# Routing of a mixture of experts: logits in four column groups, folded as they are turned, and the token rows turned back beside the picking

## The chip, the cores and the metric

The kernel runs on one core of a Trainium2 chip. The time is the device time of one execution in microseconds (us), the median of several. All data is 32-bit floating point. The names of the engines in the profile are PE (TensorE; PEld is its loading of weights), ACT (ScalarE), DVE (VectorE), POOL (GpSimd) and SP (SyncE).

## The reference

The program is two transformer layers over 256 latent and 256 context tokens of 1024 features, and then two hybrid layers over the 256 latent ones. Each of the first two layers ends in a mixture of 16 experts. This is the part that the change touches:

```python
def moe(h, router_w, router_b, w1, w3, w2):
    N = h.shape[0]
    scores = jax.nn.sigmoid((h @ router_w).astype(jnp.float32))
    sel = (scores + router_b.astype(jnp.float32)).reshape(N, N_GROUPS, EXP_PER_GROUP)
    group_score = lax.top_k(sel, TOP_K)[0].sum(axis=-1)
    g_idx = jnp.argmax(group_score, axis=-1)
    sel_in = jnp.take_along_axis(sel, g_idx[:, None, None], axis=1)[:, 0]
    _, local = lax.top_k(sel_in, TOP_K)
    e_idx = g_idx[:, None] * EXP_PER_GROUP + local
    w = jnp.take_along_axis(scores, e_idx, axis=-1)
    w = w / w.sum(axis=-1, keepdims=True)
    comb = (jax.nn.one_hot(e_idx, N_EXPERTS, dtype=jnp.float32) * w[..., None]).sum(axis=1).astype(h.dtype)
    y = jnp.zeros_like(h)
    for e in range(N_EXPERTS):
        y = y + comb[:, e:e + 1] * ((jax.nn.silu(h @ w1[e]) * (h @ w3[e])) @ w2[e])
    return y
```

There are 4 groups of 4 experts, and each token goes to 2 experts of its best group. In the first layer all 512 tokens pass through the experts, in the second the 256 latent ones.

## The kernel before

**Stages.** The program is written as stages (`class Stage`, L110 to L148). In a stage each engine has a program of its own; each waits at its start until every engine that took part in the stages before has finished (`stage_done`), so no two stages overlap. Within a stage, engines meet through counting semaphores: `bank_full` (a PSUM bank is written), `bank_free_act` (ScalarE has emptied one), `act_out` (ScalarE has written a result). Inside one engine's program a `drain` waits until its own writes are visible.

**Layout.** `hT` holds the normalised and modulated activations with the features on the partitions: 8 tiles (`KT`) of 128 features by up to 512 tokens. `turn` (L266) turns tiles of 128x128 on TensorE, four into one PSUM bank, and ScalarE copies each bank out. A product in this data type is two MATMUL instructions in the trace, a transpose is one.

**The order around the change.** Ahead of the experts of each layer (`moe` at L452 for the first layer with `nt` = 4 tiles of tokens, `moe_narrow` at L730 for the second with `nt` = 2) stand:

1. `turned` (L438): `xn` is turned into `hT`.
2. `turn` once more: `hT` is turned back into `h_tok`, rows of tokens, in `2 * nt` banks.
3. `route` (L1051), its first stage. TensorE makes the logits in one bank for each tile of tokens: `hT` is stationary and `router_w` (128x16 for each `k`) moves, `nt * 8` products (L1088). ScalarE issues the stores of `h_tok` to `h_rows` in HBM (`keep_rows`, L482 and L760) and then takes the sigmoids (L1097). GpSimd makes small tables: `prio`, `iota`, `base`, `token` and the strict triangle `before`.
4. `route`, its second stage, on VectorE alone: some forty small steps from L1118 to L1159. They pick the best group, the best expert (`hot`) and the second (`hot2`), put their sum in `sel` (L1146), and compute the two weights.
5. `route`, its third stage. TensorE counts (L1169 and L1172): the rank of each token among those of its expert is the product of `before` with its own tile, plus the product of `ones` with each tile ahead of it; a further `nt` products give the total of each expert. VectorE (L1180 to L1199) takes from these `rank`, `first` and `passes`, the number of passes that the experts' loop makes.
6. The experts' stage. SyncE waits for `stage_done` of the routing before it requests any expert weights into the `ring` of 3 buffers. VectorE makes `picks` from `rank` (L692), TensorE multiplies them with `mine` for the indices of the tokens (L611), and GpSimd gathers the rows of each expert from `h_rows` (L637), for which it first waits on `h_stored`. Then the products run expert by expert (L585, L604).

**Elsewhere.** The modulation's products (`product`, L332) use `silu_c`, padded to 32 columns, as stationary tile. Product `k` writes the 32 partitions of PSUM that begin at `32 * (k % 4)`, so four products stand in four column groups of the array; `cond_of` (128x2, L189), a stack of four pieces of an identity, later adds the groups up (L359 and L362). At the start of the program ScalarE's queue issues the parameter loads (L205), ahead of its first activation (L407). The first product of the modulation waits for that.

The core of the counts before is:

```python
for m in range(nt):
    for b in range(m + 1):
        mm = pe.matmul(bank[0][:, m * N_EXP:(m + 1) * N_EXP], before[:, :] if b == m else ones[:, :],
                       sel[:, b, :], start=(b == 0), stop=(b == m))
for m in range(nt):
    mm = pe.matmul(bank[1][:, 0:N_EXP], ones[:, :], sel[:, m, :], start=(m == 0), stop=(m == nt - 1))
```

## Time and profile before

| what | value |
|---|---|
| median of three runs | 2834.15 us |
| lowest and highest run | 2834.11 and 2837.87 us |
| the profiled execution, its own time | 2837.68 us |
| its span | 2835.9 us |
| granted clock of TensorE, mean | 0.955 |
| DVE, ACT, POOL busy | 29%, 17%, 4% of the span |

The span is what the profiler sees of the execution; the 1.8 us around it belong to its time. The granted clock is a share of TensorE's full speed. It has two levels: 0.5 is 1.2 GHz and 1.0 is 2.4 GHz, and a value between them is a mean over a stretch with both. A timeline row gives the start, the length from the first start to the last end, and how many instructions it joins; what stands in brackets is idle time of that engine just before, and what ended it.

### The profile page before, as it was taken

What the parts mean: (1) busy time and instruction counts of PE and PEld (TensorE: products, weight loads), DVE (VectorE), ACT (ScalarE), POOL (GpSimd) and SP (SyncE); (2) the same over time, 40 slices, a digit from 0 to 9 for tenths busy, and PEclk for the clock granted to TensorE, in tenths of its full rate; (3) what the DMA queues carried; (4) which work ended last, traced back from release to release, by engine and by line L of the source; (5) the groups of instructions that cost most, each with busy time, mean ns of one, the idle gap of its engine ahead of it and who ended that gap; (6) DMA issues with size and microseconds to landing.
All of it is one profiled execution on the core that took longest, in us unless ns stands there. A gap on an engine that the chain in (4) does not pass through costs nothing.

```text
span 2835.9 us, 29978 instructions
## 1 busy us (share of the span) xinstructions
PE 2601.5 (92%) x12110; PEld 1746.6 (62%) x12110; DVE 830.0 (29%) x2043; ACT 478.9 (17%) x1010; POOL 113.2 (4%) x156
## 2 busy tenths in 40 slices
PE   5999998599997587799959999999999999999999
PEld 3465653444443245344424888888886788888884
DVE  0255321200100263111111677212210377512220
ACT  2133322111111222011110112101110111111210
POOL 0000000000000000000000000400000000400000
PEclk8999999699999797899979999999999999999999
DMA  7403483499997220999962443343443434344442
GB/s 240 127 30 104 145 294 125 152 329 330 336 334 261 101 69 15 320 384 385 380 253 95 148 137 131 139 157 120 149 162 120 153 125 143 119 149 141 149 148 96
DMA packets 299770, 517.14 MB, mean 182 GB/s; under 512 B 25072, under 2 KB 118640, under 8 KB 299632
## 3 DMA queue, kind: packets, MB, share of 16 engines
q1 hardware_dynamic: 281168, 473.87, 48.4%
q0 software_dynamic: 5824, 20.97, 2.1%
q10 hardware_dynamic: 12640, 20.37, 1.9%
q8 instruction: 97, 1.59, 0.2%
q14 instruction: 41, 0.34, 0.0%
HBM read 496.31 MB, written 18.87 MB: 182 GB/s over the span
## 4 chain that ended last, share of the span: by engine, by line
PE 85%; DMA 6%; DVE 3%; ACT 2%; ACTq 1%; issue 1%; DVEq 1%; POOL 0%; SPq 0%; POOLq 0%
PE bank L2536 32%; PE bank L585 8%; PE bank L2522 4%; DMA ring<-in_exp_w 4%; PE bank L604 4%; PE bank L1541 3%; PE bank L866 3%; PE bank L1551 3%; PE bank L2656 3%; PE bank L2671 3%; PE bank L1927 2%; PE bank L342 2%; PE bank L871 2%; PE bank L2021 1%; PE bank L2630 1%; PE bank L2620 1%
## 5 line engine op out<-in xcount | busy, mean ns | idle before, releaser
L2536 PE MATMUL bank<-hT,ring 128*128 128x256 f32 x3456 | 763.4, 381 | 7.0 <-DVE hT L2862 7.0
L2536 PEld LDWEIGHTS bank<-hT,ring 128*128 128x128 f32 x3456 | 655.1, 191 | 97.9 <-issue 10.4
L585 PE MATMUL bank<-ring,hg 128*128 128x512 f32 x512 | 226.9, 597 | 1.0 <-DVE hg L686 1.0
L2977 DVE SCALAR_TENSOR_TENSOR y_conf<-y_glu,s_cw,y_conf 128x256 f32<-128x256 f32 x480 | 195.0, 478 | 0.8
L585 PEld LDWEIGHTS bank<-ring,hg 128*128 128x128 f32 x512 | 95.7, 192 | 110.1 <-issue 110.1
L3059 DVE SCALAR_TENSOR_TENSOR y_conf<-bank,s_fw,y_conf 128x255 f32<-128x255 f32 (+1 forms) x176 | 72.7, 475 | 216.3 <-ACT y_conf L2805 214.3
L866 PE MATMUL bank<-ring,hg 128*64 128x512 f32 x512 | 119.8, 610 | 10.1 <-DMA ring<-in_exp_w 7.0
L2522 PE MATMUL bank<-ring,hT 128*128 128x512 f32 (+1 forms) x320 | 122.1, 545 | 6.6 <-DVE hT L2862 6.6
L604 PE MATMUL bank<-ring,hidT 128*128 128x512 f32 x256 | 112.6, 592 | 1.3 <-ACT hidT L667 1.3
L2522 PEld LDWEIGHTS bank<-ring,hT 128*128 128x128 f32 x320 | 57.6, 196 | 71.6 <-issue 69.9
L1541 PE MATMUL bank<-ring,hT 128*128 128x384 f32 (+2 forms) x256 | 97.9, 526 | 2.9 <-ACTq L132 2.9
L1551 PE MATMUL bank<-ring,hT 128*128 128x384 f32 (+2 forms) x256 | 95.8, 517 | 0.0
L604 PEld LDWEIGHTS bank<-ring,hidT 128*128 128x128 f32 x256 | 48.6, 190 | 62.2 <-issue 60.7
L866 PEld LDWEIGHTS bank<-ring,hg 128*64 128x64 f32 x512 | 36.6, 139 | 73.9 <-issue 69.7
L686 DVE COPY hg<-bank 128x512 f32<-128x512 f32 x32 | 20.7, 687 | 207.9 <-PE bank L571 207.9
L342 PE MATMUL bank<-ring,silu_c 128*32 128x512 f32 x384 | 52.1, 664 | 30.0 <-ACT silu_c L407 23.7
L2656 PE MATMUL bank<-y_gates,ring 128*128 128x256 f32 x352 | 76.5, 379 | 0.0
L2671 PE MATMUL bank<-ring,y_gates 128*128 128x512 f32 x176 | 75.7, 592 | 0.0
L2805 ACT ACTIVATE y_conf<-bank,s_fb,s_fw 128x256 f32<-128x256 f32 x88 | 42.5, 564 | 193.8 <-PE bank L2536 193.8
L278 PE MATMUL bank<-ident,xn 128*128 128x128 f32 x80 | 14.5, 364 | 64.4 <-DVEq L132 64.4
L1541 PEld LDWEIGHTS bank<-ring,hT 128*128 128x128 f32 x256 | 48.7, 210 | 39.1 <-issue 22.3
L2656 PEld LDWEIGHTS bank<-y_gates,ring 128*128 128x128 f32 x352 | 66.9, 190 | 9.1
(444 smaller groups left out, 2843.6 us busy)
## 6 DMA issues: line engine op xcount, KB each, us to landing
ring<-in_exp_w SPq DMA_DIRECT2D x48, 2048.0 KB, 10.5
ring<-in_exp_w SPq DMA_DIRECT2D x96, 1024.0 KB, 8.6
ring<-in_ada_w SPq DMA_DIRECT2D x24, 2048.0 KB, 10.2
ring<-in_w_in SPq DMA_DIRECT2D x24, 2048.0 KB, 7.9
ring<-in_w_up SPq DMA_DIRECT2D x44, 1024.0 KB, 6.6
ring<-in_w_in SPq DMA_DIRECT2D x32, 1024.0 KB, 7.7
ring<-in_w_down SPq DMA_DIRECT2D x8, 2048.0 KB, 8.0
moe_y<-ye ACTq DMA_DIRECT2D x16, 512.0 KB, 8.8
```

The source lines that it names most:

```text
L342: mm = pe.matmul(bank[self.rows_banks[f % n]][g:g + 32, :], silu_c[:, k, :], wt[:, k, :], start=(k < 4), stop=(k >= 4))
L585: mm = pe.matmul(b[0:SLOTS, :], hg[:, e % 2, k, :], w[:, k, :], start=(k == 0), stop=(k == KT - 1))
L604: mm = pe.matmul(bank[5 + half][0:SLOTS, :], hidT[:, k, :], w[:, k, half * COLS:(half + 1) * COLS], start=(k == 0), stop=(k == 3))
L866: pe.matmul(bank[2][SA * a:SA * a + SA, :], hg[:, e % 2, kk, 0:SA], w[a][:, k, :], start=(kk == 0), stop=(kk == KT - 1))
L1541: pe.matmul(DENSE[g % 2][:, 0:width], hT[:, k, i * P:(i + 1) * P], wt[:, k, 0:width], start=(k == 0), stop=False)
L1551: mm = pe.matmul(DENSE[g % 2][:, 0:width], hT[:, k, i * P:(i + 1) * P], wt[:, k, 0:width], start=False, stop=(k == KT - 1))
L2522: mm = pe.matmul(pair(s)[i][:, 0:qkv_w[c]], h[:, k, i * P:(i + 1) * P], w[:, k, :], start=(k == 0), stop=(k == KT - 1))
L2536: mm = pe.matmul(b, w[:, k, j * P:(j + 1) * P], moving(k), start=(k == 0), stop=(k == KT - 1))
L2656: mm = pe.matmul(bank[O_BANKS[t]][:, 0:S_LAT], w[:, k, j * P:(j + 1) * P], hid[:, k0 + k, :], start=(k0 + k == 0), stop=(k0 + k == FT - 1))
L2671: mm = pe.matmul(b[:, :], hid[:, k0 + k, i * P:(i + 1) * P], w[:, k, :], start=(k0 + k == 0), stop=(k0 + k == FT - 1))
L2977: ins = dve.scalar_tensor_tensor(conf[:, f, :], src, cw[:, f, k:k + 1], conf[:, f, :], ALU.mult, ALU.add)
L3059: ins = dve.scalar_tensor_tensor(a, b[j // 2][:, lo:lo + S_LAT - sh], cw[:, t, k:k + 1], a, ALU.mult, ALU.add)
```

## The change

Where `moe` and `moe_narrow` turned the rows back in a stage of their own, this now happens inside `route`, whose three stages become one. In it, by engine:

- **TensorE** makes the logits the other way round: `router_w`, padded with zeros to 32 columns, is stationary, and `hT` moves with all the tokens at once; product `k` goes to column group `k % 4`. The four partial sums lie in one bank as 4 x 32 rows by tokens. ScalarE copies them to `part`, and `nt` products with `part` stationary and `fold` moving (a stack of four 32x16 pieces of an identity) add the four up and turn them in the same step. Then come the `2 * nt` banks of turned rows, and then, when VectorE has signalled `route_picked` behind the sum of `hot` and `hot2`, the counts: one product with `before` over all tiles, `nt - 1` products with `ones` that add tile `b` to all tiles behind it, and one that gives the totals of each tile apart.
- **ScalarE** starts with an activation of one column (`warm`) that loads the table of the sigmoid. It copies `part`, takes one sigmoid over all tiles, and then copies the turned rows, with a store behind each second copy.
- **VectorE** does the same steps in the same order, except that the pair of `first` stands between the steps of the weights, and that it adds the tiles' totals up itself (`total`).
- `fold` (128x16) replaces `cond_of` (128x2), which becomes its first two columns. `router_w` is loaded padded. `h_tok` and the tables of `route` are kept until the experts' stage is over.

```diff
-    cond_of = sb(ctx, "cond_of", [P, 2])
-    router_w = sb(ctx, "router_w_sb", [P, KT, N_EXP])
+    fold = sb(ctx, "fold_sb", [P, N_EXP])
+    cond_of = fold[:, 0:2]
+    router_w = sb(ctx, "router_w_sb", [P, KT, 32])
...
-            for m in range(nt):
-                for k in range(KT):
-                    mm = pe.matmul(bank[m][:, 0:N_EXP], hT[:, k, m * P:(m + 1) * P], router_w[:, k, :],
-                                   start=(k == 0), stop=(k == KT - 1))
+            for k in range(KT):
+                g = 32 * (k % 4)
+                mm = pe.matmul(bank[0][g:g + 32, 0:n_tok], router_w[:, k, :], hT[:, k, 0:n_tok], start=(k < 4), stop=(k >= 4))
+            mm.then_inc(bank_full.sem, 1)
+            pe.wait_ge(act_out.sem, a0 + 1)
+            for m in range(nt):
+                mm = pe.matmul(bank[1][:, m * N_EXP:(m + 1) * N_EXP], part[:, m * P:(m + 1) * P], fold[:, :],
+                               start=True, stop=True)
             mm.then_inc(bank_full.sem, 1)
+            for j in range(2 * nt):
+                if j >= 4:
+                    pe.wait_ge(bank_free_act.sem, b0 + j - 3)
+                for i in range(4):
+                    mm = pe.transpose(bank[2 + j % 4][:, i * P:(i + 1) * P], hT[:, (j % 2) * 4 + i, (j // 2) * P:(j // 2 + 1) * P],
+                                      ident[:, :])
+                mm.then_inc(bank_full.sem, 1)
+            pe.wait_ge(route_picked.sem, g0 + 1)
+            every = sel[:, :, :].rearrange("p m e -> p (m e)")
+            pe.matmul(bank[6][:, 0:nt * N_EXP], before[:, :], every, start=True, stop=False)
+            for b in range(nt - 1):
+                pe.matmul(bank[6][:, (b + 1) * N_EXP:nt * N_EXP], ones[:, :],
+                          sel[:, b:b + 1, :].to_broadcast([P, nt - 1 - b, N_EXP]), start=False, stop=(b == nt - 2))
+            pe.matmul(bank[7][:, 0:nt * N_EXP], ones[:, :], every, start=True, stop=True).then_inc(bank_full.sem, 1)
 
         @st.scalar
         def _(act):
-            keep_rows(act)
-            act.wait_ge(bank_full.sem, f0 + 1)
-            for m in range(nt):
-                act.activation(sc[:, m, :], bank[m][:, 0:N_EXP], ACT.Sigmoid)
-        bank_full.n += 1
-        st.end()
-        st = Stage()
+            act.activation(warm[:, :], ones[:, 0:1], ACT.Sigmoid)
+            act.wait_ge(bank_full.sem, f0 + LOGITS)
+            act.activation(part[:, :], bank[0][:, 0:n_tok], ACT.Copy).then_inc(act_out.sem, 1)
+            act.wait_ge(bank_full.sem, f0 + TURNED)
+            act.activation(sc[:, :, :].rearrange("p m e -> p (m e)"), bank[1][:, 0:nt * N_EXP], ACT.Sigmoid)\
+                .then_inc(act_out.sem, 1)
+            for j in range(2 * nt):
+                act.wait_ge(bank_full.sem, f0 + TURNED + j + 1)
+                act.activation(h_tok[:, j // 2, (j % 2) * COLS:(j % 2 + 1) * COLS], bank[2 + j % 4][:, :], ACT.Copy)\
+                    .then_inc(bank_free_act.sem, 1)
+                if j % 2:
+                    m = j // 2
+                    act.wait_ge(bank_free_act.sem, b0 + j + 1)
+                    act.dma_start(h_rows[m * P:(m + 1) * P, :], h_tok[:, m, :]).then_inc(h_stored, 16)
...
-            both = sel[:, :, :]
-            dve.tensor_tensor(both, hot[:, :, :], hot2[:, :, :], ALU.add)
-            dve.drain()
+            dve.tensor_tensor(sel[:, :, :], hot[:, :, :], hot2[:, :, :], ALU.add).then_inc(route_picked.sem, 1)
...
             dve.tensor_tensor(best[:, :], wgt[:, :, 0], wgt[:, :, 1], ALU.add)
+            for c, h in enumerate((hot, hot2)):
+                dve.tensor_tensor(spot[:, c, :, :], h[:, :, :], base[:, :].unsqueeze(1).to_broadcast([P, nt, N_EXP]),
+                                  ALU.mult)
             dve.drain()
             dve.reciprocal(gs[:, 0:nt], best[:, :])
+            for c in range(2):
+                dve.tensor_reduce(first[:, :, c], spot[:, c, :, :], AX, ALU.add)
             dve.drain()
             dve.tensor_tensor(wgt[:, :, :], wgt[:, :, :], bc(gs[:, 0:nt], 2), ALU.mult)
-        st.end()
...
+            dve.wait_ge(bank_full.sem, f0 + RANKED)
...
-            dve.tensor_reduce(few[:, 0:1], bank[1][:, 0:N_EXP], AX, ALU.max)
+            dve.tensor_reduce(total[:, :], bank[7][:, 0:nt * N_EXP].rearrange("p (m e) -> p e m", m=nt), AX, ALU.add)
...
+            dve.tensor_reduce(few[:, 0:1], total[:, :], AX, ALU.max)
```

TensorE in the first layer, from the turning back to the experts, before. A row stands for one product, or for the number behind the x:

```order
L278 MATMUL bank<-ident,hT 128x128 [waits stage_done]
L278 MATMUL bank<-ident,hT 128x128 x31
L127 UNCONDITIONAL_BRANCH
L1088 MATMUL bank<-router_w_sb,hT 128x16 [waits stage_done]
L1088 MATMUL bank<-router_w_sb,hT 128x16 x31
L127 UNCONDITIONAL_BRANCH
L1169 MATMUL bank<-r_sel,r_before 128x16 [waits stage_done]
L1169 MATMUL bank<-r_sel,ones 128x16
L1169 MATMUL bank<-r_sel,r_before 128x16
L1169 MATMUL bank<-r_sel,ones 128x16 x2
L1169 MATMUL bank<-r_sel,r_before 128x16
L1169 MATMUL bank<-r_sel,ones 128x16 x3
```

After this come one more row of L1169 and the four products of L1172. The same place on TensorE in the changed kernel:

```order
L1084 MATMUL bank<-hT,router_w_sb 32x512 [waits stage_done]
L1084 MATMUL bank<-hT,router_w_sb 32x512 x7
L1088 MATMUL bank<-fold_sb,r_part 128x16 [waits act_out]
L1088 MATMUL bank<-fold_sb,r_part 128x16 x3
L1095 MATMUL bank<-ident,hT 128x128 x16
L1095 MATMUL bank<-ident,hT 128x128 [waits bank_free_act]
...
L1100 MATMUL bank<-r_sel,r_before 128x64 [waits route_picked]
L1102 MATMUL bank<-r_sel,ones 128x48
L1102 MATMUL bank<-r_sel,ones 128x32
L1102 MATMUL bank<-r_sel,ones 128x16
L1104 MATMUL bank<-r_sel,ones 128x64
```

The turning has moved from ahead of the logits to between the folding and the counts. 32 products of the logits have become 8 and 4, and 14 of the counts have become 5.

ScalarE in the same place of the changed kernel:

```order
L1108 ACT_TABLE_LOAD
L1108 ACTIVATE r_warm<-ones 128x1 [waits stage_done]
L1110 ACTIVATE r_part<-bank 128x512 [waits bank_full]
L1112 ACTIVATE r_sc<-bank 128x64 [waits bank_full]
L1116 ACTIVATE h_tok<-bank 128x512 [waits bank_full] x2
L1121 DMA moe_h<-h_tok 128x1024 [waits bank_free_act]
```

The last two rows stand there four times. The stores, which stood ahead of the sigmoids in one block, are now spread between the copies behind the sigmoid.

## Rows read from the trace of the kernel before

**Rows 1.** The page, part 1: busy us (share of span) xinstructions, by engine.

```profile
PE 2601.5 (92%) x12110; PEld 1746.6 (62%) x12110; DVE 830.0 (29%) x2043; ACT 478.9 (17%) x1010; POOL 113.2 (4%) x156
```

**Rows 2.** Windows: per engine busy us (x instructions), then PEclk, DMA share, GB/s.

```profile
490.00:492.00 2.00, 2.00 (x10) 2.00 (x11) 0.00 (x0) 0.94 (x3) 0.00 (x0) 0.50 0.00 0
...
494.00:496.00 2.00, 1.08 (x10) 0.85 (x8) 0.00 (x0) 2.00 (x5) 0.00 (x0) 1.00 0.00 0
...
498.50:500.00 1.50, 1.45 (x13) 1.45 (x14) 0.00 (x0) 0.69 (x2) 0.00 (x0) 0.95 0.00 0
...
500.00:502.00 2.00, 2.00 (x11) 2.00 (x10) 0.00 (x0) 1.55 (x4) 0.00 (x0) 0.50 0.00 0
...
554.00:556.00 2.00, 2.00 (x3) 0.97 (x4) 0.45 (x4) 0.00 (x0) 0.32 (x1) 0.50 1.04 383
```

**Rows 3.** Timeline, first layer: start us, us, engine, line, op, out<-in, count [idle before].

```profile
498.55 5.38 PE L278 MATMUL bank<-ident,hT 128*128 128x128 f32 x32 [3.47 <-ACTq L132]
...
501.07 0.60 ACT L286 ACTIVATE h_tok<-bank 128x512 f32<-128x512 f32 x1 [0.20 <-PE bank L278]
...
504.70 12.07 PE L1088 MATMUL bank<-router_w_sb,hT 128*128 128x16 f32 x64 [0.77 <-ACTq L132]
...
517.28 0.23 DVE L1118 TENSOR_TENSOR r_sel<-r_sc,router_b_sb 128x64 f32<-128x64 f32 x1 [27.52 <-ACTq L132]
...
523.76 0.23 DVE L1146 TENSOR_TENSOR r_sel<-r_hot 128x64 f32<-128x64 f32 x1
...
530.21 1.87 PE L1172 MATMUL bank<-r_sel,ones 128*128 128x16 f32 x8
...
532.18 0.36 DVE L1180 TENSOR_TENSOR r_spot<-bank,r_hot 128x64 f32<-128x64 f32 x2 [6.35 <-PEq L132]
...
533.12 0.36 DVE L1187 TENSOR_TENSOR r_spot<-r_hot,r_base 128x64 f32<-128x64 f32 x2
...
533.98 0.15 DVE L1195 TENSOR_SCALAR r_few<-r_few 128x1 f32<-128x1 f32 x1
...
535.37 0.15 DVE L1199 CAST passes<-r_few 128x1 int32<-128x1 f32 x1
...
543.26 1.16 POOL L637 DMA_INDIRECT hs<-moe_h,idx  x1 [0.57 <-issue]
```

**Rows 4.** Timeline, second layer, the same columns.

```profile
1113.19 3.68 PE L278 MATMUL bank<-ident,hT 128*128 128x128 f32 x16 [0.96 <-ACTq L132]
...
1124.94 0.19 DVE L1118 TENSOR_TENSOR r_sel<-r_sc,router_b_sb 128x32 f32<-128x32 f32 x1 [16.47 <-ACTq L132]
...
1130.77 0.19 DVE L1146 TENSOR_TENSOR r_sel<-r_hot 128x32 f32<-128x32 f32 x1
...
1135.11 0.29 DVE L1180 TENSOR_TENSOR r_spot<-bank,r_hot 128x32 f32<-128x32 f32 x2 [2.51 <-PEq L132]
...
1137.57 0.15 DVE L1199 CAST passes<-r_few 128x1 int32<-128x1 f32 x1
```

**Rows 5.** Timeline of TensorE: the modulation's products in four column groups.

```profile
23.72 3.64 PE L342 MATMUL bank<-ring,silu_c 128*32 128x512 f32 x16 [23.72 <-ACT silu_c L407]
...
398.23 1.92 PE L342 MATMUL bank<-ring,silu_c 128*32 128x512 f32 x16
```

**Rows 6.** Timeline at the start: ScalarE's queue issues the parameter loads.

```profile
4.96 2.42 ACTq L205 DMA_DIRECT2D router_w_sb<-in_router_w  x1
...
7.40 4.89 ACTq L205 DMA_DIRECT2D router_b_sb<-in_router_b  x1
```

**Rows 7.** Timeline of ScalarE: a table load and the activation behind it.

```profile
484.72 1.28 ACT L254 ACT_TABLE_LOAD   x1
...
486.02 0.30 ACT L254 ACTIVATE stats<-stats,eps_col 128x4 f32<-128x4 f32 x1
```

**Rows 8.** Line L482, stores of the token rows: issue ns (min/median/max), then landing.

```profile
L482 ACTq DMA_DIRECT2D moe_h<-h_tok x4: 346/626/1474, 504.7 to 507.1; - x4
...
DMA to landing us min/median/max: 3.5/4.3/4.9
```

More of the change, by code:

```diff
@@ L474, in moe @@
             passes = sb(mem, f"passes{l}", [P, 1], mybir.dt.int32)
[L475 removed]
             h_stored = sem("h_stored")
[L477 to L484 removed]
+            route(l, mem, h_rows, h_stored, rank, wgt, first, mine, iota, passes, nt, SLOTS)
             picks = sb(mem, f"picks{l}", [P, 2 * nt, SLOTS])
@@ L752, in moe_narrow @@
             passes = sb(mem, f"passes{l}", [P, 1], mybir.dt.int32)
[L753 removed]
             h_stored = sem("h_stored")
[L755 to L762 removed]
+            route(l, mem, h_rows, h_stored, rank, wgt, first, mine, iota, passes, nt, S)
             picks = sb(mem, f"picks{l}", [P, 2 * nt, S])
@@ L1049, in moe_narrow, with route @@
                 used_at[chunks[0] - RING + j] = (ring_free, 1)
-    def route(l, mem, rank, wgt, first, mine, iota, passes, nt, keep_rows, slots):
-        f0, a0 = bank_full.n, act_out.n
+    def route(l, mem, h_rows, h_stored, rank, wgt, first, mine, iota, passes, nt, slots):
+        f0, a0, b0 = bank_full.n, act_out.n, bank_free_act.n
+        r0, g0 = route_made.n, route_picked.n
+        n_tok = nt * P
+        h_tok = sb(mem, f"h_tok{l}", [P, nt, D])
+        part = sb(mem, f"r_part{l}", [P, n_tok])
+        warm = sb(mem, f"r_warm{l}", [P, 1])
         sc = sb(mem, f"r_sc{l}", [P, nt, N_EXP])
@@ L1063, in route @@
         few = sb(mem, f"r_few{l}", [P, 3])
+        total = sb(mem, f"r_total{l}", [P, N_EXP])
         base = sb(mem, f"r_base{l}", [P, N_EXP])
@@ L1095, in _ @@
-            act.wait_ge(bank_full.sem, f0 + 1)
-            for m in range(nt):
-                act.activation(sc[:, m, :], bank[m][:, 0:N_EXP], ACT.Sigmoid)
-        bank_full.n += 1
-        st.end()
-        st = Stage()
+            act.activation(warm[:, :], ones[:, 0:1], ACT.Sigmoid)
[4 more added lines that the diff above has]
+                .then_inc(act_out.sem, 1)
@@ L1184, in _ @@
                 dve.tensor_reduce(rank[:, :, c], spot[:, c, :, :], AX, ALU.add)
-            dve.drain()
-            for c, h in enumerate((hot, hot2)):
-                dve.tensor_tensor(spot[:, c, :, :], h[:, :, :], base[:, :].unsqueeze(1).to_broadcast([P, nt, N_EXP]),
-                                  ALU.mult)
-            dve.memset(few[:, 1:2], 1.0)
-            dve.drain()
-            for c in range(2):
-                dve.tensor_reduce(first[:, :, c], spot[:, c, :, :], AX, ALU.add)
+            dve.tensor_reduce(few[:, 0:1], total[:, :], AX, ALU.max)
             for q in range(1, -(-nt * P // slots)):
@@ L1199, in _ @@
             dve.tensor_copy(passes[:, :], few[:, 1:2])
-        bank_full.n += 1
+        bank_full.n += RANKED
+        act_out.n += 2
+        bank_free_act.n += 2 * nt
+        route_made.n += 1
+        route_picked.n += 1
         st.end()
```

46 lines of the change are left out of this document (13 added, 33 removed).

## The prediction

> **What bounds the kernel now.** I read the page first. TensorE is busy for 92% of the span [rows 1], so most of the kernel is a stream of products, and anything that TensorE does not do inside that stream is on the path. The change sits in two short stretches that are not part of that stream: the routing ahead of the experts of the first layer (498.55 to 535.52 us) and of the second (1113.19 to 1137.72 us). I then took the timeline of both. Each is a relay with one runner: TensorE turns the modulated rows back (32 transposes, 5.38 us), then multiplies for the logits (64 records, 12.07 us), then VectorE picks from 517.28 us, TensorE counts until 532.08 us, and VectorE finishes with the cast at 535.37 us that takes 0.15 us [rows 3]. The second layer runs the same relay with half the tokens [rows 4]. Nothing overlaps with it: the expert weights are requested by SyncE only when the routing stages are over, and everything later waits for them. So what these stretches lose, the whole kernel loses, one for one.
>
> The windows give the granted clock. It is 0.50 at 490 us while TensorE turns, 1.00 at 494 us, 0.95 at the start of the routing and 0.50 from 500 us [rows 2]. 0.50 is 1.2 GHz and 1.00 is 2.4 GHz. So a price must be taken at the right level.
>
> **First layer, what stands there before.** From 498.55 to 535.52 us: 37.0 us [rows 3].
>
> **Logits.** 32 products of 128x16 (two records each, 12.07 us) become 8 products of 32x512, four column groups at a time. The same form exists in the modulation: sixteen records take 1.92 us in one place and 3.64 us in another [rows 5]. In the first 1.45 us the clock is high [rows 2]; that does 1.45/1.92 = 76% of the work, and the rest costs 0.24 x 3.64 = 0.9 us: 2.3 us. Bounds: 1.9 and 3.6.
>
> **Copy, folding, sigmoid.** ScalarE copies 128x512, 0.60 us [rows 3], with two hand-overs of 0.05: 0.7 us. Four folding products are eight records, as the eight of L1172 in 1.87 us [rows 3]: 1.9 us. Bounds 0.9 and 1.9, the lower for a high clock, at which half would do. Four sigmoids stand between 516.77 and 517.28 us, with both hand-overs; one of 128x64 lies between a quarter of that and 0.6: I take 0.3 us. VectorE starts 2.3 + 0.7 + 1.9 + 0.3 = 5.2 us into the stretch, where it now needs 18.7. The table for the sigmoid is loaded by a dummy activation under the logits: 1.28 us [rows 7] plus some 0.2 is less than 2.3, so I cost it at nothing.
>
> **Picking.** From L1118 to L1146 nothing changes: 523.76 - 517.28 = 6.5 us [rows 3].
>
> **From L1146 to the cast.** Now 535.52 - 523.76 = 11.8 us, of which VectorE is idle 6.35 for the counts [rows 3]: 5.4 of its own work. The pair of `first` (533.12 to 533.98, 0.86 us [rows 3]) moves up between other steps, where it needs no waits for its predecessor: about 0.5. The sum over tiles (`total`) adds 0.15. That makes 5.4 - 0.86 + 0.5 + 0.15 = 5.2 us if VectorE need not wait. It is ready for the counts 532.18 - 6.35 - 523.76 = 2.1 us after L1146 begins, plus the 0.5: 2.6 us. The counts are now 5 products, ten records, 10/8 x 1.87 = 2.3 us at the low clock [rows 3]; started 0.3 after L1146 begins (its own 0.23 and the hand-over) they end at 2.6 to 2.7. At the high clock they are earlier. So they hide, just. If they had kept 28 records, 6.1 us, they would not.
>
> **The turning moves behind the logits** and is costed at nothing. Its cover is the picking. It starts 4.9 us in; The 32 transposes took 5.38 us here [rows 3], and at the second layer's slower pace of 16 in 3.68 [rows 4] they would take 7.4. So they end 10.3 to 12.3 us in, and the counts cannot start before 5.2 + 6.5 + 0.3 = 12.0 in any case. TensorE works in order, so this is the place to watch: at the slow pace the cover is gone and the counts come 0.3 us late. I take the middle, 11.3, since the clock rose under transposes once already (below). Half of the turns also wait for a bank that ScalarE frees. ScalarE takes 0.60 per copy, and issues a store behind each second one, 0.35 to 1.47 us [rows 8]: even four copies and a slow issue (3.9 us) are over long before the last turn's bank is wanted. The last store is issued by 12.3 + 0.6 + 1.5 = 14.4 us and lands 4.9 us later at worst [rows 8], before the gather that needs it, which comes 7.7 us after the routing's end [rows 3].
>
> **Sum, first layer:** 5.2 + 6.5 + 5.2 = 16.9 us for 37.0. Gain 20.1 us.
>
> **Second layer** (24.5 us, from 1113.19 to 1137.72 [rows 4]). Logits: 256 columns at the low clock, half of 3.64 = 1.8 [rows 5]. Copy 0.4 and hand-overs 0.1; folding four records, 1.0; sigmoid and hand-overs 0.3: 3.6. Here the dummy activation ends 1.5 us in, still ahead of the copy. Picking 1130.77 - 1124.94 = 5.8. From L1146: 1137.72 - 1130.77 = 6.95, less the idle 2.51 [rows 4], less 0.7 for the moved pair, plus 0.4 for it in its new place, plus 0.1 for `total`: 4.2. The 16 turns end by 3.3 + 3.7 = 7.0 us in, ahead of the pick. The counts (six records, 1.4 us) end before VectorE is ready. Sum 3.6 + 5.8 + 4.2 = 13.6, **gain 10.9 us**.
>
> **Start of the program.** The router weights come padded from 16 to 32 columns, and a table of 128x16 takes the place of one of 128x2. ScalarE's queue issues these ahead of its first activation, and the issues behind the router weights stall: 2.42 and 4.89 us [rows 6]. The number of pieces is the same and each is twice as long. Bounds: no cost, and a doubling of both stalls, 7.3 us. I take 0.2 us, near the low end, since 64 KB more is small beside the 2 MB pieces of weights that share the engines.
>
> **Total:** 20.1 + 10.9 - 0.2 = 30.8 us. The profiled execution took 2837.68 us, so its like would take 2806.9; that execution is 3.5 us above the median of the runs, 2834.15, from which the forecast is **2803.4 us**.
>
> **A rule weighed.** While TensorE did nothing but transposes, the granted clock rose from 0.50 to 1.00 [rows 2]. The Trainium skill ("TensorE: Matmul & The Clock Gate", Part 4) says that transposes do not count as busy and leave the clock low. By that rule the moved turns run low to their end, the counts behind them too, and I would add 0.4 us; the trace speaks against it.
>
> **Rivals.**
> (a) The clock stays low through turns and counts. The turns then end 12.3 us in and the counts 2.4 later, at 14.7, where VectorE is ready at 11.7 + 2.6 = 14.3: 0.4 us, so 2803.8 us, chance 0.06. For: 0.50 at 500 us. Against: 1.00 at 494 us [rows 2]. The rule of the Trainium skill quoted above would give this case.
> (b) The dummy activation is dear: a pause of the length of a load follows it, so that ScalarE is ready 2.8 us in. That is 0.5 us late in the first layer and 1.0 in the second: 2804.9 us, chance 0.03. Against: the load at 484.72 us ends at 486.00, and the activation starts at 486.02 [rows 7]. The Trainium skill ("ScalarE: Activation LUTs", What ACT_TABLE_LOAD costs) gives a load of 1283 ns and 1380 ns of drain; the row agrees with the first and shows no second.
> (c) The issue queue stalls twice as long at the start: 7.3 us for 0.2, so 2810.5 us, chance 0.04.
> (d) The column groups do not run together, so the change does not do what it says. Then each record takes as long as a set of four does now, 1.92/4 = 0.5 us at best and 3.64/4 = 0.9 at worst [rows 5]: three fast and thirteen slow ones make 13.3 us for 2.3 in the first layer, and sixteen of half the length 7.3 for 1.8 in the second. That is 16.5 us more, 2819.9 us, chance 0.02. Against: sixteen such records in 1.92 us [rows 5].
> (e) Slower. TensorE does less in the routing, so the clock is lower and the expert loop of the first layer starts at 1.2 GHz and stays there. At 554 us it is at 0.50 already [rows 2], and rises soon after. Each us that products spend at half the clock costs half a us, so 62 us more of it eat the gain: that is the point from which it decides. With 150 us it is 2803.4 + 75 = 2878 us. Against: TensorE idles there before and after the change alike, and the loop lifts the clock by its own work. Chance 0.02.
>
> **How the numbers follow.** The forecast as reasoned has 0.83. Its own range: the logits, folding and hand-overs may be 1.5 us off to either side in total; every later stage starts 20 or 31 us earlier, so the places where the clock steps can fall differently, and the low stretch at 554 us alone is worth 2 us; and the three runs shown differ by 3.7 us. So 2799.5 to 2808. To reach case (b) and (c) the range goes to 2811: **2799.5 to 2811**. About 0.2% (5.7 us) is what a measurement of this kernel can tell. Cases (a) to (d) are all faster by more than that: faster 0.96. Same, 0.02, is what a partial (e) or something unseen would give; slower 0.02.
>
> **What would show it.** The routing of the first layer should take some 17 us from its first product to the cast, that of the second some 14. VectorE's first step should follow the first product by 5.2 and 3.6 us. The logits' sixteen records should take about 2.3 and 1.8 us. VectorE's idle time ahead of L1190 should be under 0.3 us; if it is longer, the turns or the counts are late. The first product of the modulation should still start near 23.7 us. The forecast is wrong if VectorE waits over 1 us for the counts, if the stretches are as forecast but the total is not, or if the start has moved.

## The result, and the profile after

The changed kernel takes 2805.2 us (median of 6 runs, 2802.03 to 2813.57), the kernel before 2834.13 us (6 runs, 2828.81 to 2837.87). The ratio is 0.9904, with a 95% interval of 0.9887 to 0.9922: 27 us faster, between 22 and 32 (27.2 us lie between the means of the runs, 28.9 between the medians). The forecast was 2803.4 us in a range of 2799.5 to 2811, so 30.8 us faster. The profiled execution took 2805.25 us with a span of 2803.5; that of before had a span of 2835.9. The two spans are 32.4 us apart.

The page's first part, which answers to [rows 1]:

```profile
PE 2578.9 (92%) x12036; PEld 1721.9 (61%) x12036; DVE 829.0 (30%) x2045; ACT 479.7 (17%) x1010; POOL 112.9 (4%) x156
```

TensorE has 12036 records for 12110 and the same share of the span. The timeline of the first layer's routing, which answers to [rows 3]:

```profile
499.34 2.65 PE L1084 MATMUL bank<-hT,router_w_sb 128*32 128x512 f32 x16 [3.58 <-ACTq L133]
...
499.34 1.28 ACT L1108 ACT_TABLE_LOAD   x1
...
500.64 0.20 ACT L1108 ACTIVATE r_warm<-ones 128x1 f32<-128x1 f32 x1
...
502.69 1.89 PE L1088 MATMUL bank<-fold_sb,r_part 128*128 128x16 f32 x8 [0.70 <-ACT r_part L1110]
...
504.41 5.05 PE L1095 MATMUL bank<-ident,hT 128*128 128x128 f32 x32
...
504.87 0.22 DVE L1142 TENSOR_TENSOR r_sel<-r_sc,router_b_sb 128x64 f32<-128x64 f32 x1 [4.52 <-ACT r_sc L1112]
...
511.35 0.23 DVE L1169 TENSOR_TENSOR r_sel<-r_hot 128x64 f32<-128x64 f32 x1
...
511.63 0.43 PE L1100 MATMUL bank<-r_sel,r_before 128*128 128x64 f32 x2 [2.16 <-DVE r_sel L1169]
...
512.54 0.41 PE L1104 MATMUL bank<-r_sel,ones 128*128 128x64 f32 x2
...
513.68 0.35 DVE L1190 TENSOR_TENSOR r_spot<-bank,r_hot 128x64 f32<-128x64 f32 x2
...
516.13 0.15 DVE L1202 CAST passes<-r_few 128x1 int32<-128x1 f32 x1
...
524.01 1.16 POOL L631 DMA_INDIRECT hs<-moe_h,idx  x1 [0.57 <-issue]
```

The routing runs from 499.34 to 516.28 us, 16.94 us for 36.97. VectorE's first step (504.87) follows the first product by 5.53 us. The row at 513.68 has no bracket: VectorE does not wait for the counts, which were over at 512.95. The same of the second layer, for [rows 4]:

```profile
1095.37 1.07 PE L1084 MATMUL bank<-hT,router_w_sb 128*32 128x256 f32 x16 [0.96 <-ACTq L133]
...
1096.78 0.37 ACT L1110 ACTIVATE r_part<-bank 128x256 f32<-128x256 f32 x1
...
1098.09 0.19 DVE L1142 TENSOR_TENSOR r_sel<-r_sc,router_b_sb 128x32 f32<-128x32 f32 x1 [1.69 <-ACT r_sc L1112]
...
1103.92 0.19 DVE L1169 TENSOR_TENSOR r_sel<-r_hot 128x32 f32<-128x32 f32 x1
...
1107.68 0.15 DVE L1202 CAST passes<-r_few 128x1 int32<-128x1 f32 x1
```

1095.37 to 1107.83 us: 12.46 us for 24.53. The windows, which answer to [rows 2] (engines' busy us, then PEclk, DMA share, GB/s):

```profile
499.30:502.00 2.70, 2.65 (x16) 0.42 (x16) 0.06 (x1) 1.49 (x2) 0.75 (x5) 0.70 0.00 0
...
504.40:507.00 2.60, 2.60 (x13) 2.60 (x14) 1.70 (x11) 1.42 (x3) 0.00 (x0) 0.50 0.00 0
...
507.00:509.50 2.50, 2.46 (x22) 2.23 (x20) 1.88 (x9) 1.67 (x4) 0.00 (x0) 0.96 0.57 233
...
1095.30:1096.50 1.20, 1.07 (x16) 0.42 (x16) 0.06 (x1) 1.12 (x1) 0.76 (x5) 1.00 0.00 0
...
1099.00:1101.30 2.30, 2.27 (x11) 1.88 (x9) 1.62 (x10) 1.55 (x3) 0.00 (x0) 0.53 0.10 41
...
534.60:537.50 2.90, 2.88 (x4) 1.34 (x5) 0.51 (x5) 0.00 (x0) 0.45 (x1) 0.50 1.05 386
...
538.00:541.00 3.00, 3.00 (x8) 1.33 (x7) 0.00 (x0) 0.00 (x0) 0.00 (x0) 1.00 0.88 332
```

While TensorE only turned rows, the clock rose from 0.50 (504.4) to 0.96 (507.0). In the second layer the logits met a clock of 1.00, and under the turns behind them it fell: 0.53 from 1099.0 to 1101.3 us. The start, for [rows 6], and the stores, for [rows 8]:

```profile
5.05 2.51 ACTq L207 DMA_DIRECT2D router_w_sb<-in_router_w_wide  x1
...
7.59 4.86 ACTq L207 DMA_DIRECT2D router_b_sb<-in_router_b  x1
...
22.46 1.28 ACT L409 ACT_TABLE_LOAD   x1 [22.46 <-issue]
...
24.07 3.64 PE L344 MATMUL bank<-ring,silu_c 128*32 128x512 f32 x16 [24.07 <-ACT silu_c L409]
```

```profile
L1121 ACTq DMA_DIRECT2D moe_h<-h_tok x6: 326/330/345, 507.0 to 1101.9; - x6
...
DMA to landing us min/median/max: 2.6/2.6/2.6
```

The links of the relay, each as the distance between the starts of the rows that bound it, the last one up to the end of the cast:

| link, us | 1st layer: before | forecast | after | 2nd layer: before | forecast | after |
|---|---|---|---|---|---|---|
| turning back, bare | 6.15 | 0 | 0 | 4.39 | 0 | 0 |
| first logit product to VectorE's first step | 12.58 | 5.2 | 5.53 | 7.36 | 3.6 | 2.72 |
| picking | 6.48 | 6.5 | 6.48 | 5.83 | 5.8 | 5.83 |
| from the sum of the picks to the cast | 11.76 | 5.2 | 4.93 | 6.95 | 4.2 | 3.91 |
| sum | 36.97 | 16.9 | 16.94 | 24.53 | 13.6 | 12.46 |

The routings give 20.03 and 12.07, together 32.1 us: 10.5 by the turning, 11.7 by the logits, 9.9 behind the sum of the picks. The two spans are 32.4 us apart.

### The profile page after: what moved, and what is told of

It reads as the page before. It is cut to its first block, busy times and chain, and to the rows that moved or that the text cites. A ratio compares the mean times of both kernels' runs of the same rounds, so it can differ in the third digit from the quotient of the medians.

```text
span 2803.5 us, 29818 instructions
## 1 busy us (share of the span) xinstructions
PE 2578.9 (92%) x12036; PEld 1721.9 (61%) x12036; DVE 829.0 (30%) x2045; ACT 479.7 (17%) x1010; POOL 112.9 (4%) x156
## 4 chain that ended last, share of the span: by engine, by line
PE 85%; DMA 6%; DVE 3%; ACT 2%; ACTq 1%; issue 1%; DVEq 1%; POOL 0%; SPq 0%; POOLq 0%
PE bank L2543 33%; PE bank L579 8%; PE bank L2529 4%; DMA ring<-in_exp_w 4%; PE bank L598 4%; PE bank L1548 3%; PE bank L852 3%; PE bank L1558 3%; PE bank L2663 3%; PE bank L2678 3%; PE bank L1934 2%; PE bank L344 2%; PE bank L857 2%; PE bank L2028 2%; PE bank L2637 1%; PE bank L2627 1%
## 5 line engine op out<-in xcount | busy, mean ns | idle before, releaser
L852 PE MATMUL bank<-ring,hg 128*64 128x512 f32 x512 | 119.7, 610 | 11.3 <-DMA ring<-in_exp_w 8.0
## 6 DMA issues: line engine op xcount, KB each, us to landing
ring<-in_exp_w SPq DMA_DIRECT2D x48, 2048.0 KB, 10.2
```

The source lines that it names most:

```text
L852: pe.matmul(bank[2][SA * a:SA * a + SA, :], hg[:, e % 2, kk, 0:SA], w[a][:, k, :], start=(kk == 0), stop=(kk == KT - 1))
```

## The experiments

Twelve kernels ran, each beside the kernel before on the same chip; the chips differ between them, and the kernel before took 2830.5 to 2834.1 us there. The execution was cut at the same rows in each trace: the start of the first product (or transpose) of a routing, and the end of its cast. The code behind the first, the third and the fifth column is the same in all these kernels, but for the parameter loads, which are a little narrower in the kernel before, and the first 45 us of three kernels (marked *).

| kernel | up to 1st routing | 1st routing | between | 2nd routing | rest | median of all its runs |
|---|---|---|---|---|---|---|
| before | 498.55 | 36.97 | 577.67 | 24.53 | 1698.18 | 2834.13 |
| changed | 499.34 | 16.94 | 579.09 | 12.46 | 1695.67 | 2805.2 |
| changed, again | 496.67 | 17.28 | 581.82 | 12.48 | 1697.95 | 2807.89 |
| old logits | 499.03 | 24.58 | 581.79 | 14.98 | 1693.02 | 2817.16 |
| turning ahead | 495.15 | 21.98 | 580.85 | 15.37 | 1698.35 | 2813.93 |
| old counts | 500.86 | 18.19 | 579.39 | 14.05 | 1698.51 | 2812.63 |
| turning twice | 498.06 | 18.99 | 577.30 | 12.86 | 1697.09 | 2804.02 |
| no dummy | 499.01 | 17.27 | 581.93 | 12.90 | 1700.79 | 2813.7 (1 run) |
| one group | 495.37 | 22.40 | 577.35 | 14.75 | 1696.13 | 2807.77 (1 run) |
| late signal | 498.18 | 19.68 | 579.11 | 14.14 | 1700.09 | 2813.0 (1 run) |
| late signal, old counts | 500.56 | 21.63 | 579.51 | 15.89 | 1696.61 | 2816.0 (1 run) |
| narrow load * | 497.04 | 17.10 | 581.86 | 12.47 | 1701.63 | 2811.84 (1 run) |
| parameters by GpSimd * | 496.06 | 17.07 | 578.84 | 12.47 | 1695.66 | 2802.47 |
| start reordered * | 497.05 | 17.22 | 581.93 | 12.48 | 1695.62 | 2804.72 |

Code that did not change differs by 5.7 us before the first routing (unmarked rows), 4.6 between and 8.6 behind (all rows). That is more than most single effects here. So the verdicts below rest on the two routings, which repeat within 0.4 us where the clock is the same, and the medians only have to agree.

**The scatter.** The changed kernel once more.

> The changed kernel once more, for the scatter. Theory: the two routings take 16.9 us and, by the level of the clock at its start, 12.5 or about 13.6 us; the median is 2803 to 2808 us, and any larger distance from the first profile lies in stretches whose code did not change. Rival (the total scatters with the routings): the routings themselves differ by over 2 us from those of the first profile.

Measured: 2807.89 us (2802.19 to 2808.51), ratio to before 0.9902 (0.9885 to 0.9918). The routings differ from the first profile by 0.34 and 0.02 us, and the other three stretches by -2.7, +2.7 and +2.3. The theory holds. What differs inside the first routing is the pace of TensorE:

```profile
502.08 6.39 PE L1095 MATMUL bank<-ident,hT 128*128 128x128 f32 x32
```

The same turns took 5.05 us in the first profile, and the same logits 2.99 us for 2.65. The turns ended 11.8 us in, not 10.1, and 0.8 us ahead of the finished sum of the picks (509.25 us), not 2.1; VectorE did not wait in either.

**Logits as they were.**

```diff
-                mm = pe.matmul(bank[0][g:g + 32, 0:n_tok], router_w[:, k, :], hT[:, k, 0:n_tok], ...)
+            for m in range(nt):
+                for k in range(KT):
+                    mm = pe.matmul(bank[1][:, m * N_EXP:(m + 1) * N_EXP], hT[:, k, m * P:(m + 1) * P],
+                                   router_w[:, k, 0:N_EXP], start=(k == 0), stop=(k == KT - 1))
...
```

> The changed kernel, with the logits alone as they were: 32 and 16 products with the activations stationary, no partial sums and no folding. Theory (each link of the relay is worth what its rows show, and all behind it moves rigidly): VectorE's first step comes 12.1 us after the first product in place of 5.5 in the first layer, and 7.1 in place of 2.7 in the second, so the two routings take 6.6 and 4.4 us more, and the kernel 11 us more than the changed one, 2816 us. Rival (the old products are slow only because TensorE's clock was low there, and now it is high): 64 records at 0.11 us are 7 us, 32 are 3.5, so 2 us more in all.

TensorE's timeline in both layers:

```profile
499.03 12.88 PE L1084 MATMUL bank<-router_w_sb,hT 128*128 128x16 f32 x64 [3.57 <-ACTq L133]
...
1105.40 4.96 PE L1084 MATMUL bank<-router_w_sb,hT 128*128 128x16 f32 x32 [0.98 <-ACTq L133]
```

Measured: 2817.16 us, ratio 0.995 (0.9934 to 0.9967), 12 us above the changed kernel. The routings take 7.64 and 2.52 us more, 10.2 in all. VectorE's first step comes 13.18 and 5.23 us in, where the theory had 12.1 and 7.1. In the first layer it holds but for 1.1 us. In the second it does not: the old products took 4.96 us where they had taken 7.01 before, at a higher clock, so part of the rival is true there. Of the 4.6 us by which this link is shorter in the second layer's profiles, 2.1 came with the clock and not with the edit.

**Are the four groups what makes them quick?**

```diff
-                g = 32 * (k % 4)
-                mm = pe.matmul(bank[0][g:g + 32, 0:n_tok], ..., start=(k < 4), stop=(k >= 4))
+                mm = pe.matmul(bank[0][0:32, 0:n_tok], ..., start=(k == 0), stop=(k == KT - 1))
...
```

> The changed kernel with all eight logit products in one column group, accumulated there, and the folding done over 32 rows. It measures what the four groups are worth. Theory (four groups run at the same time): sixteen records then take 16/4 times the spacing of a set, 7.0 us at the high clock and 13.9 at the low one for 512 tokens, 3.5 or 7.0 for 256, in place of 2.65 and 1.07: 4.5 to 11 us more in the first layer, 2.4 to 6 in the second. Rival (products with a 32-column stationary tile are quick by themselves): the same 2.65 and 1.07.

```profile
495.37 8.75 PE L1083 MATMUL bank<-hT,router_w_sb 128*32 128x512 f32 x16 [2.07 <-ACTq L133]
...
1095.12 3.64 PE L1083 MATMUL bank<-hT,router_w_sb 128*32 128x256 f32 x16 [1.26 <-ACTq L133]
```

Measured: 8.75 us for 2.65 and 3.64 for 1.07. The routings are 5.46 and 2.29 us longer (one run). The groups do run at the same time, a factor of 3.4 in the second layer, where the granted clock was 1.00 in both kernels. That closes rival (d).

**Turning back ahead of the logits.** The transposes and ScalarE's copies stand in a stage of their own again, the stores behind the sigmoid.

```diff
+        turn(lambda i, k: hT[:, (k % 2) * 4 + i, (k // 2) * P:(k // 2 + 1) * P],
+             lambda k: h_tok[:, k // 2, (k % 2) * COLS:(k % 2 + 1) * COLS], 4, 2 * nt)
...
```

> The changed kernel, with the turning back of the rows again in a stage of its own ahead of the logits, and the stores behind the sigmoid. Theory: the turning is fully hidden now and fully bare here, so the distance from the first transpose to the first logit product, 6.1 us in the first layer and 4.4 in the second, comes on top: 10.5 us more than the changed kernel, 2815.5 us. Rival (the turns beside the picking slow ScalarE or the counts, so that part of them is paid today): the picking and the counts here get shorter by over 1 us, and the kernel is less than 9 us slower.

```profile
495.15 5.38 PE L280 MATMUL bank<-ident,hT 128*128 128x128 f32 x32 [3.62 <-ACTq L133]
...
501.34 1.92 PE L1087 MATMUL bank<-hT,router_w_sb 128*32 128x512 f32 x16 [0.81 <-ACTq L133]
...
514.53 0.36 DVE L1180 TENSOR_TENSOR r_spot<-bank,r_hot 128x64 f32<-128x64 f32 x2 [0.29 <-PE bank L1100]
...
1097.98 1.97 PE L280 MATMUL bank<-ident,hT 128*128 128x128 f32 x16 [0.96 <-ACTq L133]
```

Measured: 2813.93 us, ratio 0.9939 (0.9922 to 0.9955), 8.7 above the changed kernel; the routings take 5.04 and 2.91 us more, 8.0 for the 10.5 expected. The total falls below the rival's 9, but for another reason: picking takes the same 6.47 and 5.83 us, and the counts are longer, not shorter. What is missing is the clock that these stretches met: the first layer's logits took 1.92 us for 2.65, and the second layer's turns took 1.97 us where they take 3.6 now. That the turns ahead raised it isn't shown: in "late signal, old counts", with no turns ahead, the first layer's logits took 1.92 us as well. So the turning was fully hidden, and bare it costs what the clock makes of it.

**How much cover it has.** Every transpose done twice.

```diff
-                for i in range(4):
+                for i in [0, 1, 2, 3] * 2:
```

> The changed kernel with every transpose of the turning done twice into the same place. Theory: the cover is the picking, and what goes beyond it is paid through the counts, since TensorE works in order. The turns of the first layer take 10 us in place of 5.05 and end some 2.8 us after the pick, so the counts start that late and VectorE idles about 2.1 us ahead of them; in the second layer 7.1 us in place of 3.6, ending 0.5 us after the pick, 0.3 us of idle time. The routings take 2.0 to 2.8 us more in all. Rival (turning delays nothing whatever its length): 0. Rival (all of it is paid): 8.5 us more.

First layer, TensorE and VectorE:

```profile
503.35 10.00 PE L1095 MATMUL bank<-ident,hT 128*128 128x128 f32 x64
...
510.28 0.23 DVE L1169 TENSOR_TENSOR r_sel<-r_hot 128x64 f32<-128x64 f32 x1
...
513.19 0.33 PE L1100 MATMUL bank<-r_sel,r_before 128*128 128x64 f32 x2
...
514.45 0.36 DVE L1190 TENSOR_TENSOR r_spot<-bank,r_hot 128x64 f32<-128x64 f32 x2 [1.76 <-PE bank L1104]
```

The turns end at 513.35, 2.8 us after the sum of the picks is ready (510.28 + 0.23), and VectorE idles 1.76 us, for the 2.1 expected. The routing is 2.05 us longer, of 5 us that were added; 0.22 of it are slower logits. In the second layer the doubled turns took 4.96 us and hid, with no idle time; its 0.40 us more come from a slower folding. The sum, 2.45 us, lies in the theory's 2.0 to 2.8, but by luck in part: 1.8 us of it are the turning's, 0.6 the clock's. The median, 2804.02, shows nothing of it.

**Counts as they were**, but started early.

```diff
-            pe.matmul(bank[6][:, 0:nt * N_EXP], before[:, :], every, start=True, stop=False)
+            for m in range(nt):
+                for b in range(m + 1):
+                    pe.matmul(bank[6][:, m * N_EXP:(m + 1) * N_EXP], before[:, :] if b == m else ones[:, :],
+                              sel[:, b, :], start=(b == 0), stop=(b == m))
...
```

> The changed kernel with the counts alone as they were: 14 and 5 products (28 and 10 records) in place of 5 and 3. Theory: VectorE is ready for them 2.1 us after they start, so only what goes beyond is paid. 28 records take 3.6 us at the high clock and 6.1 at the low one: VectorE idles 1.6 to 4.1 us ahead of the step that reads them in the first layer, and 0 to 0.6 in the second. The kernel is 1.5 to 4.5 us slower than the changed one. Rival (the counts are hidden in any form, the single stage is what removed the wait): idle time of 0 and no difference.

VectorE's step that reads the counts, in both layers:

```profile
516.57 0.35 DVE L1191 TENSOR_TENSOR r_spot<-bank,r_hot 128x64 f32<-128x64 f32 x2 [1.50 <-PE bank L1104]
...
1110.62 0.29 DVE L1191 TENSOR_TENSOR r_spot<-bank,r_hot 128x32 f32<-128x32 f32 x2 [0.56 <-PE bank L1104]
```

Idle 1.50 and 0.56 us; from the sum to the cast 6.39 and 4.47 us for 4.93 and 3.91. That is 2.0 us for both, the low end; the first layer's idle time is 0.1 below its range. The routings are 2.84 us longer, the rest because the second layer's logits met the low clock (1.93 us). The median, 2812.63 (ratio 0.9925, 0.9908 to 0.9941), is 7.4 above the changed kernel: between the two profiles 4.7 us lie in stretches whose code did not change.

**The early start alone, and both undone.** The signal for the counts moved behind the last step of the weights; the second kernel has the old counts as well.

```diff
-            dve.tensor_tensor(sel[:, :, :], hot[:, :, :], hot2[:, :, :], ALU.add).then_inc(route_picked.sem, 1)
+            dve.tensor_tensor(sel[:, :, :], hot[:, :, :], hot2[:, :, :], ALU.add)
...
-            dve.tensor_tensor(wgt[:, :, :], wgt[:, :, :], bc(gs[:, 0:nt], 2), ALU.mult)
+            dve.tensor_tensor(wgt[:, :, :], wgt[:, :, :], bc(gs[:, 0:nt], 2), ALU.mult).then_inc(route_picked.sem, 1)
```

> The changed kernel with the signal for the counts moved from behind the sum of the two picks to behind the last step of the weights, so that five and three products start when VectorE has nothing left to do. Theory (the early start is worth more than the fewer products): VectorE idles for the whole of the counts, 1.4 to 2.5 us in the first layer and 1.0 to 1.8 in the second by the clock, so the stretches from the sum to the cast take 6.3 to 7.4 and 4.9 to 5.7 us in place of 4.93 and 3.91. Rival (the fewer products are what was gained, the start matters little): under 0.5 us each.

> Both undone: the late signal and the 14 and 5 products of the kernel before. Theory: VectorE idles 3.6 to 6.3 us in the first layer and 1.4 to 2.5 in the second, and the stretches from the sum to the cast take 8.5 to 11.2 and 5.3 to 6.4 us; of the 6.8 and 3.0 us that the change took off these stretches (11.76 to 4.93, 6.95 to 3.91) this gives back nearly all. The two undone together cost more than the early start alone by the 18 and 4 records, 2.3 to 4 us and 0.5 to 1 us. Rival (the barriers between the stages were what cost): clearly less, and what is missing is the barriers'.

VectorE in the first layer, of the first kernel and of the second:

```profile
515.27 0.35 DVE L1190 TENSOR_TENSOR r_spot<-bank,r_hot 128x64 f32<-128x64 f32 x2 [2.49 <-PE bank L1104]
```

```profile
519.72 0.35 DVE L1191 TENSOR_TENSOR r_spot<-bank,r_hot 128x64 f32<-128x64 f32 x2 [6.25 <-PE bank L1104]
```

With the late signal alone the stretches from the sum to the cast take 7.50 and 5.59 us, 2.57 and 1.68 more. With both undone they take 11.14 and 6.32, 6.21 and 2.41 more, nearly the 11.76 and 6.95 of before. The theories hold: late, the full length of the counts is paid; early, only what exceeds some 2 us. So the two parts are not additive. Fewer products save 2.0 us behind an early signal (above) and 4.4 us behind a late one (11.14 - 7.50 + 6.32 - 5.59). The early start saves 4.3 us with the new products and 6.6 with the old ones (11.14 - 6.39 + 6.32 - 4.47), part of it through the clock: the new counts took 2.40 us when late and 1.32 when early. Both undone, 0.6 us in each layer are still not given back. VectorE's own steps, without the idle time, take 4.89 and 3.91 us where the kernel before has 5.41 and 4.44: the pair of `first` stands between other steps, and the `drain` behind the sum is gone. The wait itself is only 0.1 us shorter (6.25 for 6.35, 2.41 for 2.51), and no more than that can be due to the barrier ahead of the counts: the rival is refuted.

Undone one by one, the turning, the logits, and the counts with their start give back 8.0, 10.2 and 8.6 us, 26.8 of the 32.1. Of the other 5.3 us the 1.2 above stand behind the sum of the picks; the rest goes with the clock that the logits and the turns met in these profiles.

**The dummy activation.** Its line taken out.

> The changed kernel without the dummy activation that loads the table of the sigmoid. Theory: the load then runs between the copy of the partial sums and the sigmoid, under the folding products. In the first layer these take 1.9 us for its 1.28, so nothing changes there; in the second the load ends some 0.3 us behind the folding at the high clock, and the copy gains up to 0.3 us because it no longer stands behind the dummy. Both routings stay within 0.4 us of 16.9 and 12.5 us. Rival (the load waits for the folding with the sigmoid): 1.3 us more in each.

ScalarE in the second layer:

```profile
1099.81 1.28 ACT L1111 ACT_TABLE_LOAD   x1
...
1101.10 0.20 ACT L1111 ACTIVATE r_sc<-bank 128x32 f32<-128x32 f32 x1
```

The activation starts 0.01 us behind the load's end. In the first layer the sigmoid follows the folding at once, as with the dummy; its 0.33 us more are mostly the logits' (2.92 us for 2.65). In the second the load is the last thing to end, and VectorE's first step comes 3.12 us in for 2.72. The dummy is worth 0.4 us there, and the load has no pause behind it, which closes rival (b).

**The price at the start.** The router weights loaded 16 wide, the other columns zeroed on the chip.

> The changed kernel with the router weights loaded 16 columns wide, the rest zeroed on the chip, to price the start term alone. Theory (the wider pieces cost time in ScalarE's queue): the first product comes at 23.7 us as in the kernel before, in place of 24.07. Rival (the 0.35 us are the scatter of that queue from run to run): it stays near 24.1.

```profile
23.69 3.49 PE L345 MATMUL bank<-ring,silu_c 128*32 128x512 f32 x16 [23.69 <-ACT silu_c L410]
```

23.69 us, as the 23.72 of the kernel before; the ten unmarked kernels with wide pieces lie at 23.92 to 24.22 us. So the wide load costs some 0.3 us, on two narrow runs against ten. It does not sit in the stalls (2.60 and 4.85 us here, 2.51 and 4.86 with wide pieces).

**A try at a faster kernel.** The rows of the start show that ScalarE's own issues hold it until 22.46 us. They were moved to GpSimd:

```diff
-        load(act, params_landed,
+
+    def load_params(eng):
+        load(eng, params_landed,
...
+    @block.gpsimd
+    def _(pool):
+        load_params(pool)
```

> The changed kernel with the parameter loads at the start issued from GpSimd's queue in place of ScalarE's (all but the conditioning, the folding table and the activations). It is a try at a faster kernel, out of the row in which ScalarE's issues hold its first activation until 22.46 us. Theory (the issues gate the first product): the first product of the modulation starts at 7 to 10 us in place of 24.07, the weights then gate the next ones, the first transposes start 8 to 15 us earlier than 45.2, and the kernel takes 2790 to 2797 us. Rival (the transfers themselves gate, since 10 MB must land first at 400 GB/s, that is 25 us): under 3 us gained.

```profile
5.15 0.93 POOL L207 DMA_DIRECT2D router_w_sb<-in_router_w_wide  x1
...
6.06 0.58 POOL L207 DMA_DIRECT2D router_b_sb<-in_router_b  x1
...
14.09 3.64 PE L350 MATMUL bank<-ring,silu_c 128*32 128x512 f32 x16 [14.09 <-DMA ring<-in_ada_w]
...
21.18 1.06 ACT L260 ACTIVATE xn_first<-x 128x1024 f32<-128x1024 f32 x1 [12.06 <-DMA x<-in_ctx]
...
27.63 3.64 PE L350 MATMUL bank<-ring,silu_c 128*32 128x512 f32 x16 [9.90 <-ACT ada_part_first L378]
```

The first product starts 10 us earlier, at 14.09 us, released by its weights. But ScalarE copies its result only behind the squares, which wait for the activations (21.18 us), so the second starts at 27.63. Measured: 2802.47 us (2801.0 to 2807.08), ratio 0.9894 (0.9877 to 0.991). That is 2.7 us below the changed kernel, where the rival had under 3, but it is not shown to come from the start. The first transposes begin at 42.23 us, and in the ten kernels whose first product waits until 24 us they begin anywhere between 40.91 and 45.21 us. So the theory's 8 to 15 us are refuted, and of its mechanism only the first half came true: the first product is freed, the second is not. A last version copies the first product ahead of the squares:

```diff
-                on_scalar(act)
-                for f in range(4):
-                    first.copy(act, f)
+                first.copy(act, 0)
+                for m in (0, 1):
+                    act.activation(xn[:, m, :], x[:, m, :], ACT.Square, ...)
+                first.copy(act, 1)
...
```

> e6_params_pool with ScalarE's work at the start in another order: it copies the first product of the modulation before it waits for the activations, and the second between two of the squares. Theory (with the issues gone, the row of the second product, 27.63 us, shows that it waited for a copy that stood behind the squares): the second product starts by 19 us if its weights have landed, the third by 26 us, and the first transposes start 4 to 6 us earlier than in e6_params_pool. The kernel takes 2793 to 2799 us, below the kernel before and the changed one. Rival (the weights of the second and third product land at about 20 and 26 us, so the transfers gate): 1 to 3 us gained, 2799 to 2802 us.

```profile
17.66 0.60 ACT L378 ACTIVATE ada_part_first<-bank 128x512 f32<-128x512 f32 x1 [8.70 <-PE bank L350]
...
25.06 3.64 PE L350 MATMUL bank<-ring,silu_c 128*32 128x512 f32 x16 [7.46 <-DMA ring<-in_ada_w]
```

Now the second product waits for its weights until 25.06 us. The rival's mechanism holds: the transfers gate, and two of the squares came behind the copy that waited for it. Its price does not: it had 1 to 3 us gained, and the first transposes begin at 43.82 us, 1.6 us later than in the kernel above. Measured: 2804.72 us (2803.63 to 2806.08), ratio 0.9895 (0.9879 to 0.9912). Both intervals overlap with the changed kernel's. Neither is shown to beat it.

## Why the prediction was right

- **One runner at a time, so the loss is one for one.** Right in kind: each experiment's edit showed in its routing. Whether all that follows moves along can be told from the totals to several us only. The routings gave 32.1 us, and the spans differ by 32.4. That these agree to 0.3 us is luck, since the three unchanged stretches differ by -0.8, -1.4 and +2.5 us; the changed kernel's second profile gives 31.7 and 29.7.
- **Logits 2.3 and 1.8 us.** 2.65 and 1.07, inside the bounds for the first and below the forecast for the second. The second was priced at 1.2 GHz, and the clock was 1.00. This and the folding behind it (0.62 us for 1.0) are the mis-sized terms of the sum; the copy with its hand-overs, 0.76 us for 0.5, took some of it back. Where the clock was low there ("Counts as they were"), the logits took 1.93 us, and the routing, less its 0.56 us of idle time, 13.5 us, which is the forecast's 13.6.
- **Folding 1.9, sigmoid 0.3.** 1.89 us for the folding (502.69 to 504.58) and 0.29 from there to VectorE's first step at 504.87. Right.
- **From the sum to the cast 5.2 and 4.2.** 4.93 and 3.91. The pair of `first` cost 0.50 in its new place, as priced (0.99 us from L1177 to L1186, where the kernel before had 0.49). What the sum left out is the `drain` behind L1146, which the change takes away: L1177 starts 1.26 us behind L1169, where L1155 started 1.42 behind L1146, and that is 0.16 of the 0.27 us.
- **The counts hide, just.** They hid by 0.7 us (512.95 to 513.68), since the clock was high. VectorE was ready 2.33 us behind the start of the sum, not 2.6. So at the low clock ("Turning back ahead", counts of 2.40 us) they did not quite hide, and VectorE idled 0.29 us, about the bound that the text gave.
- **The turning hides.** In the first profile it ended 10.1 us in (509.46), just below the 10.3 of the best case and 2.1 us ahead of the pick. That isn't always so. Of the nine kernels in the table whose logits and turns are those of the changed one, three ended the turns 10.1 us in, five 11.8 us in ("changed, again" among them), only 0.6 to 0.8 us ahead of the pick, and one 7.5. The forecast's 11.3 lies among them. It hid each time, and doubling it showed where that ends.
- **The start, 0.2 us.** About 0.3. The stalls did not grow with the pieces (2.51 and 4.86 us for 2.42 and 4.89), which closes rival (c).
- **The rule on transposes**, rival (a): refuted. In the first layer the clock rose under them here too, and the counts ran at the high level in both profiles of this kernel. The Trainium skill ("TensorE: Matmul & The Clock Gate", Part 4) says otherwise, and the measurement decides. They do not hold the clock up in every place either: in the second layer it fell from 1.00 to 0.53 while TensorE folded and turned.
- **Rival (e).** It did not come: the expert loop started low (0.50 up to 537.5 us) and was at 1.00 from 538.0 us.
- **The total.** 32.4 us between the profiles and 27 (22 to 32) between the runs. The interval holds the forecast's 30.8. The unchanged stretches scatter by more than lies between these two, so the median says no more than that.

## What to carry to other kernels

Where engines take turns, price each link from its row and ask what of it could start earlier: here starting the counts sooner was worth 4 to 7 us, and making them shorter 2 to 4, the less the more of the other was already done. A short step moved under a longer one of another engine costs nothing only up to that cover, and the cover depends on the clock, so state it in us at both levels. When single edits are worth 2 or 3 us in 2800, compare the stretch that they touch in the traces; the total hides them.

## What the runs showed of the hardware

- TensorE's clock level at a given instruction is not a property of the kernel. In two profiles of the changed kernel the first layer's turns took 5.05 and 6.39 us, and over all kernels in which they stand there once 3.97 (granted clock 1.00) to 6.56 us. The same code ahead of the first routing took 495.15 to 500.86 us; how much of that is the clock's isn't shown.
- The clock rose while TensorE did nothing but transposes: from 0.50 to 1.00 in the kernel before, behind 11 us in which it had idled, and from 0.50 to 0.96 in the first layer here. In the second layer it fell from 1.00 to 0.53 under the folding and the turns. The transposes of the kernel before, at 490 us of [rows 2], with the idle time ahead of them:

```profile
489.85 5.24 PE L278 MATMUL bank<-ident,xn 128*128 128x128 f32 x32 [11.09 <-DVEq L132]
```

- Four column groups of a 32-column stationary tile gave a factor of 3.4 (3.64 to 1.07 us), not 4, for eight products of 256 columns at a granted clock of 1.00.
- In ScalarE's queue the two issues behind the load of the router weights took 4.9 us each, whether its 1024 pieces were 64 or 128 bytes long. Issued by GpSimd, each of the two took 0.6 us, and the load itself 0.93 for 2.5.
- The activation behind a table load started 0.01 to 0.02 us after its end (rows above).
